# An RWKV input projection: thirteen column blocks as plain products, or twelve channel pairs as seven block products each

## The reference

```python
n = rms_norm(x, norm1_g)
z = n @ w_in                    # 1024 -> 1304 attention columns + 1664 RWKV columns
z_attn, z_gate, z_rwkv = split(z)
q, kvs = nsa_heads(z_attn, ...)               # norm and rotation of the heads
o_attn = sparse attention (compressed, selected, window) of q, kvs
# RWKV-7 time mixing of z_rwkv
prev = z_rwkv shifted by one token            # a stored row ahead of the first
xs = z_rwkv + (prev - z_rwkv) * mu
r, k, v, xw, xa, xg = split(xs, [512, 512, 512, 32, 32, 64])
w_raw = -softplus(-(w0 + tanh(xw) @ w2)) - 0.5;  decay = exp(-exp(w_raw))
a = sigmoid(a0 + xa @ a2);  g = sigmoid(xg) @ g2
kk = normalized(k * k_k);   k = k * (1 + (a - 1) * k_a)
S_t = S decay - (S kk)(kk a)^T + v k^T;  y_t = S_t r         # per head, over the tokens
y = group_norm(y) + sum(r k r_k) v;  o_rwkv = y * g
h = x + concat(o_attn, o_rwkv) @ w_out
out = h + square(relu(rms_norm(h) @ w_up)) @ w_down
```

## Time and profile before

| | |
|---|---|
| time, 3 runs | 2077.46 us median (2077.38 to 2081.6) |
| profiled execution | 2075.0 us, its span 2073.4 us |
| PE busy | 1973.1 us, 95% of the span |
| DVE, ACT, POOL busy | 1217.8, 615.9, 659.6 us |
| granted TensorE clock | 0.986 of full speed on the mean |

### The profile page before, as it was taken

One profiled execution on the slowest core, in us unless ns is written; L12 is line 12 of the kernel. 1 busy time (PEld: TensorE's weight loads), 2 busy tenths in 40 slices (PEclk: granted clock), 3 DMA queues, 4 the chain that ended last, 5 costly groups with the idle time before them and its releaser, 6 DMA issues.

```text
span 2073.4 us, 39741 instructions
## 1 busy us (share of the span) xinstructions
PE 1973.1 (95%) x15956; PEld 1241.4 (60%) x15956; DVE 1217.8 (59%) x2486; ACT 615.9 (30%) x1428; POOL 659.6 (32%) x766
## 2 busy tenths in 40 slices
PE   8999999998988998899988999999999999999999
PEld 6445666788886784455444445656556565747473
DVE  4375564366664448777646447846465655656473
ACT  5004553233332225666644222101010101101020
POOL 3000000244432001212103004556565656555561
PEclk9999999999999997999999999999999999999999
DMA  7001012201014711000036601111111111111112
GB/s 227 0 0 27 25 31 85 85 5 25 5 37 111 195 53 57 11 6 6 6 122 204 209 1 41 41 41 41 41 41 41 41 41 41 41 41 41 41 41 86
DMA packets 96917, 115.90 MB, mean 56 GB/s; under 512 B 32252, under 2 KB 68029, under 8 KB 96671
## 3 DMA queue, kind: packets, MB, share of 16 engines
q1 hardware_dynamic: 90718, 101.82, 15.7%
q10 hardware_dynamic: 4480, 7.34, 1.3%
q0 software_dynamic: 1536, 4.20, 0.6%
HBM read 104.75 MB, written 12.64 MB: 57 GB/s over the span
## 4 chain that ended last, share of the span: by engine, by line
PE 85%; DVE 9%; issue 3%; ACT 2%; DMA 1%; ACTq 0%; POOL 0%; POOLq 0%; DVEq 0%
PE psum L1599 44%; PE psum L1602 33%; PE psum L2225 2%; PE psum L2108 1%; PE psum L2282 1%; DVE arena L2938 1%; DVE arena L3110 1%; DVE arena L3081 1%; DVE arena L2964 1%; ACT arena L1454 1%; DVE arena L3070 1%; PE psum L1947 0%; DVE arena L3083 0%; PE psum L1666 0%; ACT arena L1440 0%
## 5 line engine op out<-in xcount | busy, mean ns | idle before, releaser
L1599 PE MATMUL psum<-arena 64*64 64x64 f32 (+16 forms) x11020 | 1026.4, 299 | 51.5 <-issue 21.8
L1599 PEld LDWEIGHTS psum<-arena 64*64 64x64 f32 (+6 forms) x11020 | 596.1, 144 | 386.6 <-issue 228.8
L1602 PE MATMUL psum<-arena 128*128 128x272 f32 (+1 forms) x2464 | 753.1, 467 | 6.3 <-DVE arena L3110 5.4
L1602 PEld LDWEIGHTS psum<-arena 128*128 128x128 f32 x2464 | 459.4, 190 | 298.8 <-issue 216.2
L3132 DVE TENSOR_TENSOR arena<-arena,psum 128x512 f32<-128x512 f32 x224 | 154.1, 688 | 216.8 <-PE psum L1602 216.0
L3110 DVE TENSOR_TENSOR arena<-arena,psum 128x272 f32<-128x272 f32 x328 | 142.0, 435 | 100.0 <-PE psum L1602 97.3
L1561 ACT ACTIVATE arena<-psum 128x272 f32<-128x272 f32 x64 | 25.4, 397 | 544.7 <-PE psum L1602 544.7
L1031 POOL TENSOR_TENSOR arena<-arena 128x512 f32<-128x512 f32 x17 | 21.6, 1271 | 359.9 <-DVE arena L2774 359.9
L1098 POOL TENSOR_TENSOR arena<-arena 128x544 f32<-128x544 f32 x49 | 65.8, 1342 | 164.9 <-PE psum L1602 164.9
L1454 ACT ACTIVATE arena<-psum,arena 128x640 f32<-128x640 f32 (+7 forms) x128 | 89.0, 699 | 52.7 <-DVE arena L2938 52.5
L1025 POOL TENSOR_TENSOR arena<-arena 128x256 f32<-128x256 f32 x82 | 62.0, 757 | 113.4 <-PE psum L1599 113.1
(11 more groups left out here) (326 smaller groups left out, 2015.7 us busy)
## 6 DMA issues: line engine op xcount, KB each, us to landing
arena<-in_w_up_dram SPq DMA_DIRECT2D x7, 2048.0 KB, 8.5
arena<-in_w_down_dram SPq DMA_DIRECT2D x7, 2048.0 KB, 7.9
arena<-in_cache_slc_kv_dram SPq DMA_DIRECT2D x96, 128.0 KB, 2.6
arena<-in_cache_cmp_kv_dram SPq DMA_DIRECT2D x72, 128.0 KB, 3.5
arena<-in_x_prompt_dram SPq DMA_DIRECT2D x16, 512.0 KB, 11.8
arena<-in_cache_cmp_kv_dram ACTq DMA_DIRECT2D x56, 128.0 KB, 3.3
arena<-in_w_in_dram SPq DMA_DIRECT2D x13, 512.0 KB, 3.8
arena<-in_w_in_dram SPq DMA_DIRECT2D x2, 2048.0 KB, 18.9
```

What stands on the lines that cost most here:

```text
L1599: return nc.tensor.matmul(out, lhsT, rhs, start=start, stop=stop)
L1602: return nc.tensor.matmul(out, lhsT, rhs, start=start, stop=stop, skip_group_check=True)
```

## The change

The LoRA channel stays as it was (`lora_group`, three thirds). The other twelve are taken as six pairs of neighbouring channels, in the order k, r, k, r, v, v, and in two token halves (512 tokens, and 576 = 512 + 64): twelve "chains". In a chain the weights are a matrix of 2 x 2 blocks (two channels of 128, two halves of the 1024 inputs) and the tokens another (two halves of the inputs, two halves of the tokens). Seven block products of four matmul calls each take the place of eight:

- PE runs the products in the order 1, 2, 6, 5, 7, 3, 4 (`RW_STEPS`). Products 1, 6, 7 and 4 pile up in one bank, which the next chain's does not share, product 2 stands in a bank of its own, 5 and 3 pile up in another.
- After each product ACT (1, 6, 5, 4: `rw_copy`) or DVE (2, 7, 3: `rw_add`) reads the bank into the quarter of the result that belongs to it. PE goes on in a bank only after that reading.
- POOL makes four sums of weight blocks for each chain (`rw_sum`) and handles the columns at the seam and the last columns (`rw_edge`). DVE makes four sums of token blocks for each token half (`token_sum`), two of them in place.
- The mixing with the shifted token is now made out of SBUF: ACT copies the row shifted and times `mu` (`rw_shift`), DVE joins the two (`lerp`), a chain later.
- The twelve gate units are eight: one k channel in one token half, in the chains 1 to 4 and 7 to 10. The pieces are spread over the seven steps of a chain.
- SP loads 1 MB of weights to a chain. Some of the buffers and sums for the second token half lie in the space of the attention's projected columns `za`, so SP stores the first 1024 columns of every prompt tile to `y_prompt` in DRAM and loads them again after the last chain (8 x 512 KB each way). Keys and values are stored early.
- The last columns are turned, and taken out by ACT, inside the first period of the chunk loop.

```diff
-            def rw_group(j):
...
-                for k in range(KT):
-                    ins = mm(banks[2 + i % 3][:, 0:w], wr[m % 2][:, k, :], nt[:, k, a:a + w], k == 0, k == KT - 1)
...
+            def rw_product(e, p):
...
+                elif p in (2, 5):
...
+                        name, value = rw_read(e - 1, {2: 2, 5: 3}[p])
+                        pe.wait_ge(sem(name), value)
+                else:
+                    name, value = rw_read(e, {6: 1, 7: 6, 4: 7, 3: 5}[p])
+                    pe.wait_ge(sem(name), value)
+                if p in (6, 5, 7, 3):
+                    pe.wait_ge(sem("wl2"), rw_pool("sum", e, {6: 2, 5: 1, 7: 3, 3: 4}[p]))
...
+                for k in range(4):
+                    ins = nc.tensor.matmul(rw_bank(e, p)[:, 0:SIDES[side][1] // 2], a[:, k // 2, k % 2, :], b[:, k // 2, k % 2, :],
+                                           start=k == 0 and p in (1, 2, 5), stop=k == 3, skip_group_check=True)
+                ins.then_inc(sem("proj"), 1)
...
+            def rw_copy(e, p):
+
+                act.wait_ge(sem("proj"), rw_step(e, p))
+                dst = rw_block(e, RW_BLOCK[p])
+                nc.scalar.activation(dst, rw_bank(e, p)[:, 0:dst.shape[1]], ACT.Copy).then_inc(sem("rd_act"), 1)
...
+            def rw_add(e, p):
+
+                name, value = rw_read(e, {2: 1, 7: 5, 3: 6}[p])
+                dve.wait_ge(sem(name), value)
+                dve.wait_ge(sem("proj"), rw_step(e, p))
+                dst = rw_block(e, RW_BLOCK[p])
+                tt(dst, dst, rw_bank(e, p)[:, 0:dst.shape[1]], ALU.add).then_inc(sem("rd_dve"), 1)
+
+            def lerp(e, r):
+
+                ch, z = rw_channel(e, r), rw_rows(e, r)
+                dve.wait_ge(sem("scaled"), 3 + 2 * e + r)
+                dve.wait_ge(sem("wl2"), rw_pool("edge", e, r))
+                stt(z, z, one_mu[:, ch:ch + 1], shift_buffer(e, r), ALU.mult, ALU.add).then_inc(sem("lerped"), 1)
...
+            def rw_sum(e, n):
+
+                a11, a12, a21, a22 = (weight_block(e, r, c) for r in (1, 2) for c in (1, 2))
+                s = s_near if e < 6 else s_far
+                if n == 3:
+                    pool.wait_ge(sem(WR_IN[e % 2]), 64 * (e // 2 + 1) + 16 * (1 - e % 2))
+                    if e >= 1:
+                        pool.wait_ge(sem("proj"), rw_step(e - 1, 7))
...
+                    ins = add_two(s[3], a11, a21, ALU.subtract)
+                elif n == 1:
+                    ins = add_two(a21, a21, a22, ALU.add)
+                elif n == 2:
+                    pool.wait_ge(sem("wl2"), rw_pool("sum", e, 1))
+                    ins = add_two(s[2], a21, a11, ALU.subtract)
+                else:
+                    pool.wait_ge(sem("wl2"), rw_pool("sum", e, 2))
+                    if e >= 1:
+                        pool.wait_ge(sem("proj"), rw_step(e - 1, 3))
+                    ins = add_two(s[4], a12, s[2], ALU.subtract)
...
+            for n in range(NSTEP):
+                e, x = divmod(n, 7)
+                if RW_STEPS[x] in ADDED:
+                    rw_add(e, RW_STEPS[x])
+                if e >= 1 and x in (1, 2):
+                    lerp(e - 1, x)
...
+                if 10 <= n < 14:
+                    token_sum(1, (3, 1, 2, 4)[n - 10])
...
+            for e in range(2, NCHAIN):
+                sp.wait_ge(sem("proj"), rw_step(e - 2, RW_STEPS[-1]))
...
+                load_wr(e)
...
+            sp.wait_ge(sem("proj"), rw_step(NCHAIN - 1, RW_STEPS[-1]))
+            for t in range(PT):
+                sp.dma_start(za[:, t, 0:D_MODEL], y_prompt[0, t * P:(t + 1) * P, :]).then_inc(sem(f"x_in{t}"), 16)
...
-            pe.wait_ge(sem("lerped"), NRW)
             pe.wait_ge(sem("f_done"), UNITS)
...
+            def last_turned():
+
+                pe.wait_ge(sem("lerped"), lerped(NCHAIN - 1, 2))
+                for c in range(RC):
...
+                if n == 0:
+                    last_turned()
```

More of the change, by code:

```diff
@@ L686, in by_group @@
             return v.rearrange("p (g h d) -> p g h d", g=KVH, d=HD)
-        CHANNELS = [12, 4, 0, 5, 1, 6, 2, 7, 3, 8, 9, 10, 11]
+        LORA_CH = RC - 1
         SLOT = {c: F_R + c for c in range(RC)}
[L690 to L699, removed]
+        RW_PAIRS = (4, 0, 6, 2, 8, 10)
@@ new lines, in weight_block, with shift_buffer @@
+        def weight_block(e, r, c):
+            return weight_halves(e)[c - 1][:, :, :, P * (r - 1):P * r]
+        def shift_buffer(e, r):
+            w = SIDES[e // 6][1]
+            if e < 6:
+                return ft[:, 17 + r, 512:512 + w]
+            if e < 10:
+                return ft[:, 13 + r, 512:512 + w]
+            return region(WR0 + FAR * (r - 1), FAR)
+        RW_POOL = [("sum", 0, n) for n in (3, 1, 2, 4)]
+        for e in range(NCHAIN):
+            ahead = [("sum", e + 1, n) for n in (3, 1, 2, 4) if e + 1 < NCHAIN]
+            RW_POOL += ahead[:3] + [("edge", e, 1), ("edge", e, 2)] + ahead[3:]
@@ new lines, in _ @@
+            pool.wait_ge(sem("mp"), products_of(O0 - 1, 3))
+            for r in (1, 2):
+                nc.gpsimd.memset(shift_buffer(0, r)[:, 0:1], 0.0)
+            pool.wait_ge(sem("consts_in"), 16 * CONSTS)
+            pool.wait_ge(*once("sprev_ready"))
+            for n in (3, 1, 2, 4):
+                rw_sum(0, n)
+            for e in range(NCHAIN):
+                if e + 1 < NCHAIN:
+                    rw_sum(e + 1, 3)
+                    rw_sum(e + 1, 1)
+                    rw_sum(e + 1, 2)
+                rw_edge(e, 1)
+                rw_edge(e, 2)
+                if e + 1 < NCHAIN:
+                    rw_sum(e + 1, 4)
@@ L1292, in rows_act, with shift_out @@
+            def shift_out():
+                act.wait_ge(*once("last_turned"))
+                for q in range(4):
+                    w = min(512, ZR - 512 * q)
+                    ins = nc.scalar.activation(shift_rows[0:DEC_B + 1, q // 2, 512 * (q % 2):512 * (q % 2) + w],
+                                               banks[SHIFT_BANKS[q]][0:DEC_B + 1, 0:w], ACT.Copy)
+                ins.then_inc(once("shift_out")[0], 1)
             def rows_act(c):
@@ L2084, in _ @@
             pe.wait_ge(sem("kv_final"), TILES)
+            for t in range(PT):
+                pe.wait_ge(sem(f"x_in{t}"), spilled(t) + 16)
             pe.wait_ge(sem("rw_sstate_rows"), DEC_B)
```

589 lines of the change are left out of this document (400 added, 189 removed).

## The result

The changed kernel takes 2066.44 us (median of 10 runs, 2063.26 to 2073.81), the kernel before on the same chip 2078.56 (10 runs, 2073.94 to 2081.6): ratio 0.9947, 95% interval 0.9935 to 0.9958. It is faster by 12 us; forecast were 20.5. The time lies in the range (2052.5 to 2068), but 9 us above the forecast itself and outside the forecast's own range (2053 to 2062); the range went up to 2068 for the sake of rival A, whose price it hits (about 2066), though A is not what happened. The profiled execution took 2064.49 us, with a span of 2062.7.

A forecast was written before the change was run, and what follows sets the result against it. PE's work was taken as the bound; 2075.0 - 20.8 (removed work) - 0.7 (stage end) + 1.0 (waits) = 2054.5, and with the runs' median 2.5 above the profiled execution 2057.0 us; range 2052.5 to 2068 for 8 in 10.

The forecast's parts named there:

- rival A: In the stage's eight unit chains, late DVE or ACT readings cost 8 to 12 us: about 2066, chance 0.18.
- the removed work: PE's work in the stage falls from 220.2 to 199.4 us, 20.8 us less if PE waits nowhere.
- The price for a column: PE matmul calls cost 1.642 ns a column plus 0.014 us a call, from two call widths.
- no wait ahead of the block products: Inside a chain, readings of banks have 1.3 us of room, so PE need not wait to reuse a bank.
- B: Weight loads show openly on PE, one of 0.189 us for each of 84 products, 16 us: 2072, chance 0.05.
- C: POOL becomes the stage's bound because DVE shuts out its sums, kernel 13 us slower: 2090, chance 0.05.
- the reserve: Slack for POOL's three sums before the next chain's product 6: 3.1 us without a unit, 4.2 with one.
- Chain 1: Four token sums and a rotation crowd DVE there; it was expected late once by up to half a microsecond.
- waits inside the stage: All PE waits inside the stage together cost 1.0 us, bounds 0 and 8.
- the end of the stage: Before the chunk loop PE idles about 1.1 us instead of 1.8, 0.7 less; moving the turns gains nothing by itself.
- What comes after the stage is shifted, not changed: The program behind the stage, chunk loop onward, just starts earlier; no loss was counted there.
- Transfers ... Nothing: Weight loads, the 4 MB store to DRAM and the 4 MB reload cost no time, DMA being nearly idle.

The follow-up runs named there:

- e1: Changed kernel with every gate unit's bonus product issued one step later (the last behind the last step): 2063.29 us, ratio 0.9937 to the kernel before.
- e4: Kernel before with only its 13 turns of the last columns moved into chunk 0: 2081.86 us, ratio 1.0006 to the kernel before.
- e3: Changed kernel with the last columns turned ahead of the chunk loop again, as before the change: 2069.39 us, ratio 0.9961 to the kernel before.
- e9: Kernel before, run again without edit to see the scatter: 2078.35 us, one run.
- e10: Kernel before, a second repeat without edit to see the scatter: 2083.23 us, one run.
- e6: Changed kernel with the 4 MB window cache copy in eight pieces beside chains 3 to 10: 2064.21 us, ratio 0.9931 to the kernel before.
- e2: Changed kernel with the 4 MB reload moved from the chunk loop's start to behind chunk 8's turned keys: 2068.27 us, ratio 0.9958 to the kernel before.
- e8: Changed kernel with bonus products one step later and the window cache copy in pieces beside chains 3 to 10: 2058.93 us, ratio 0.9905 to the kernel before.
- e11: Changed kernel, run again without edit to see the scatter: 2066.38 us, one run.
- e5: Changed kernel with the reload cut from 4 MB to 64 bytes a row: 2067.37 us, ratio 0.9940 to the kernel before.
- e7: Changed kernel with the reload in eight 512 KB transfers, one behind each of chunks 0 to 7's turned keys: 2068.58 us, ratio 0.9946 to the kernel before.
- e0: Changed kernel without edit, as the control: 2065.72 us, ratio 0.9949 to the kernel before.

## Why the prediction was right or wrong

**Right: the removed work.** LoRA ended at 173.0 (forecast 173.5). From there to the last product at 359.08 are 186.05 us; forecast were 154.8 for the chains and 30.0 for the gates, 1.2 of which (the last `f_bonus`) comes behind that product: 183.6, and the measured waits of 2.7 make 186.3. The price for a column, taken from two widths, held to 0.3 us.

**Right: no wait ahead of the block products.** Rivals A and B did not occur in any trace (idle 0.0 ahead of every block product), nor C: POOL was busy for 95.8 us from 159 to 359 (forecast 60 to 75, short because the small columns of `rw_edge` cost 0.55 to 0.7 each), its sums took 1.3 to 1.8 on the mean, inside the reserve. Chain 1 did not wait either.

**Mis-sized: waits inside the stage.** 1.0 taken, 2.7 measured, in a place that was not examined: I followed the readings through DVE's queue and not `f_reads`, on which PE's bonus product waits. e1 removes the waits, and the loop starts 2.4 us sooner. This is kin to rival A, one late wait of an engine that PE depends on, but at 0.24 to 0.58 us in seven units and not 1 to 1.5 in each of eight. That the time came out at A's price (2066) is luck.

**Right: the end of the stage.** PE idle 0.94 (forecast 1.1); the first 128x512 reading at 363.5 (about 362); the turns gain nothing by themselves (e4); what they are worth in the changed kernel stays open (e3).

**Wrong: "What comes after the stage is shifted, not changed".** By the table 20.9 us were won at the loop's start; the prediction's terms make 22.1 there (20.8 less 1.0, 0.7 of idle time, 1.6 of turns that now lie inside), and the waits of 2.7 instead of 1.0 more than account for the difference. At the first mark 18.6 are left (forecast 20.5): 1.7 are the turns, and 0.5 is the share of one execution whose clock stood at 0.75 to 0.83 (chunk 0 6.66 us instead of 5.04 in the two others). By the third mark 2.9 more are gone: 21.9 us for the two periods against 19.0. There the kernel before had 6 GB/s, since its cache copy lay beside the projection and it had nothing to reload; the change put 8 MB at that place. All fourteen traces between these marks ("first wait" is that for instructions, counted from the first mark):

| trace | first to third mark, us | waits for instructions | first wait | GB/s | clock |
|---|---|---|---|---|---|
| before | 18.9 | 0 | 20.3 | 8 | 1.00 |
| e9 | 19.2 | 0 | 20.7 | 7 | 1.00 |
| e10 | 18.9 | 0 | 20.3 | 7 | 1.00 |
| e4 | 18.9 | 0 | 20.1 | 8 | 1.00 |
| e6 | 19.8 | 0.3 | 13.6 | 96 | 1.00 |
| e3 | 20.0 | 0.7 | 17.4 | 218 | 1.00 |
| e2 | 20.5 | 0.9 | 14.3 | 133 | 1.00 |
| e8 | 20.8 | 1.1 | 14.4 | 71 | 1.00 |
| e11 | 20.9 | 1.1 | 14.4 | 285 | 1.00 |
| e5 | 21.6 | 2.0 | 15.1 | 174 | 1.00 |
| after | 21.9 | 0.9 | 9.7 | 254 | 0.92 |
| e7 | 22.0 | 2.4 | 15.0 | 190 | 1.00 |
| e1 | 22.1 | 2.4 | 9.6 | 275 | 1.00 |
| e0 | 22.9 | 3.1 | 10.1 | 270 | 1.00 |

Every changed trace is longer here than every trace with the code of before, so the step fails whatever the cause. The loss follows the waits for instructions: over 19.0 it is their sum and 0.2 to 0.8 us more, but for "after", where the clock was lowered. It does not follow the traffic: e8 without the copy is as long as e11 with it, and e3 with all 8 MB in place is about as short as e6 (though more of its traffic is over by its later first mark). Moving the copy away (e6, e8) gave 2.1 and 1.0 us against the mean of three that differ by 2.0 themselves; the reload alone decides little (e5, e7), except where all of it meets the steady part (e2). So the step "Transfers ... Nothing" is refuted only for a place in the steady part. What the runs leave as the failed term is PE's supply with instructions at the loop's start, put at nothing: 0.3 to 3.1 us where the kernel before has 0. Why it differs is open. Two rivals stand untested: both transfers together (no run is without the two), and where the borders of the instruction packets fall, since the changed program has other instructions ahead of the loop and its first wait comes 3 to 11 us sooner.

**Not settled.** At the third mark 15.8 us are left and in the span 13.5. The difference of 2.3 (rounded) lies in the steady part (1.0) and behind it (1.2), both inside the scatter of three traces (5 and 3 us); the medians say 12. A lowered clock at the start of the loop stands in 6 of the 10 traces of the changed kernel and its variants, and in none of four of the kernel before. PE is less active there (36 records of 64x1, then 0.94 us idle), but e0 and e11 have the same rows and a clock of 1.00, so what decides is open.

## What to carry to other kernels

A saving in one stage is not the saving of the program: what begins earlier also begins in another place of the instruction stream, beside other transfers and at another clock. List what lay beside the stage and where it lies now, and follow every product that PE waits for, not only those of the stage's main scheme. When a loss stands beside new traffic, take the traffic away before it is called the cause: here one trace without the copy (e6) seemed to prove it, and the next (e8) was as long as with it. And an effect of a few microseconds wants more than one trace of either kernel: the first one of before was 4 us short of the mean of three.

## What the runs showed of the hardware

PE's instruction waits are regular. In the steady part of the changed kernel (and just ahead of it) the queue of instruction packets (count, MB, share) and four of PE's waits are

```profile
q8 instruction: 52, 0.85, 1.8%
```

```profile
387.30 1.74 PE L1844 MATMUL psum<-arena 64*64 64x64 f32 x71 [0.57 <-issue]
391.30 1.57 PE L1844 MATMUL psum<-arena 64*64 64x64 f32 x49 [0.68 <-issue]
395.17 1.56 PE L1844 MATMUL psum<-arena 64*64 64x64 f32 x35 [0.47 <-issue]
402.95 1.16 PE L1844 MATMUL psum<-arena 64*64 64x64 f32 x35 [1.02 <-issue]
```

52 packets in 205.2 us are one in 3.95 us, of 16 KB each; the waits end 4.0, 3.9 and twice 3.9 us apart here and last 0.2 to 1.3 us. So they keep the packets' interval, which speaks for waits at the borders of packets. The page "Advanced Engine Details and Errata" of the Trainium skill, section "ISA Cache", gives a cache line of 16 KB or 256 instructions. The packet's size agrees, and so does the count: 6635 matmul and 6630 weight load records in that stretch make 51.8 packets of 256. That a wait can grow beside bulk traffic rests on e2 alone (3.37 us beside 374 GB/s); at the loop's start, beside up to 445 GB/s, the changed kernel had none for 9.7 us, and e8 and e11 have the same waits without and with traffic. The 17.6 to 24.0 us of waits in the steady part stand in every trace of both kernels, with DMA 5% busy in most of them, and are not explained by traffic.
